# Experts with 96 rows: one strip of 64 array columns and one of 32 in place of three strips of 32

## The chip, the cores and the metric

The kernel runs on one core of a Trainium2 chip, with random inputs in float32. The metric is device time of one execution in microseconds (us), the median of several runs. TensorE (PE in the profile) is a 128x128 array; a matmul's stationary operand (loaded by LDWEIGHTS, PEld in the profile) may take all of its columns or a strip of them, and the strip is fixed by the PSUM partitions that the output goes to. In float32 each matmul of the program is two pairs of LDWEIGHTS and MATMUL in the trace, called passes here.

## The reference, cut to what matters

One decoder layer (projection, attention with forget gates, a chunked gating MLP, a merge, a mixture of experts, a gated per-layer embedding, a final norm) for 1024 prompt tokens and 64 sample tokens. The change lies in the mixture of experts:

```
# h: (1088, 1024); 32 experts in 4 groups; each token takes the best group and its best 2 of 8 experts
for each expert e, for its tokens x_e (counts differ by expert):
    y_e = (silu(x_e @ w_g[e]) * (x_e @ w_u[e])) @ w_d[e]   # 1024 -> 512 -> 1024
out[token] = sum of its two experts' rows, weighted
```

Each expert's weights are three matrices of 2 MB (w_g, w_u: 1024x512; w_d: 512x1024), so all 32 are 192 MB, read once.

## The kernel before, in words

The stages run one after the other: projection, attention, merge, routing, experts (`stage_moe`, from line 2213 on), a loop for rows that found no place (none of its matmuls is in this profile), and the final stage.

Routing ranks the experts by their number of rows. The 4 largest (`NSINGLE`) get a whole block of 128 rows. The next 12 (`NWIDE`) get 96 rows of a block each. The next six (`NSPLIT`) get 64 rows: 32 in each of two of those 12 blocks, in the strip that is left there (the lent strip). The last ten (`NHALF`) get half a block, 64 rows, two experts to a block. A block of 128 rows is a `Unit`: its list of strips (rank, first row, number of rows) covers the 128 rows. There are 21 units: 4 `single` (one strip of 128), 12 `wide` (96 rows of one expert and 32 of another) and 5 `halves` (two strips of 64).

For each unit, the block's rows are gathered, transposed on TensorE (line 2286) and kept as `XT`. The gate product, the up product (both through `product`, line 2292) and the two halves of the down product (line 2326) loop over the contraction in pieces of 128, called k-steps here (8, 8, and 2 times 4), and inside a k-step over the unit's strips:

```
for k in range(KD):
    for r, rows_ in strips(u):
        last = mm(out[rows_, :], XT[:, u % 2, k, rows_], c.ring_tile(LOAD[kind, r])[:, k, :],
                  start=(k == 0), stop=(k == KD - 1))
```

The stationary operand is the strip's rows of `XT` (128x32, 128x64 or 128x128), the moving one 128x512 of that strip's expert. So a strip of rows is a strip of array columns, and strips of one unit are different columns. A wide unit has four matmuls of 32 columns in each k-step; the first three have the same moving operand.

`ROUNDS` sets the order of the units: a single with a halves, then two wides, four times; then two rounds of two wides; then the last halves. In a round of units a and b TensorE's order is gate a, gate b, up a, up b, turn a (line 2312, transposes of the activation), transposes of the next round's rows, turn b, down a, down b. Weights come through a ring of 7 tiles of 2 MB; the SP queue issues a load (line 1837) when the last product that reads the tile's slot is done.

The code that the change touches:

Of the kernel before, what the change touches and what calls it, by code (L numbers as in the profile page):

```python
# [1765 lines left out]
STRIPE, HALF = P // 4, P // 2  # L1766
FIRST_SPLIT = NSINGLE + NWIDE
# [14 lines left out]
def wide(i, n):  # L1782

    r = NSINGLE + i + n * NSPLIT
    return Unit(r, [(r, STRIPE * q, STRIPE) for q in range(3)] + [(FIRST_SPLIT + i, 3 * STRIPE, STRIPE)])


def halves(i):
# [4 lines left out]
for _i in range(NSPLIT):  # L1793
    if _i < NSINGLE:
        ROUNDS.append([single(_i), halves(_i)])
    ROUNDS.append([wide(_i, 0), wide(_i, 1)])
# [1061 lines left out]
```

How the kernel before makes its waits and increments, by code:

```python
        @block.sync  # L213
# [2 lines left out]
                sp.dma_start(W[:, s], c.w_in[:, :, col:col + 512]).then_inc(c.w_in_sem[s], 16)  # L216
            for t in range(NP):
                sp.dma_start(X[:, t, :], c.x_prompt[t * P:(t + 1) * P, :]).then_inc(x_in[t], 16)
                if t == 1:
                    load_w(1, 2 * WA)
            sp.dma_start(X[0:NS, NP, :], c.x_sample).then_inc(x_in[NP], 16)
            load_w(0, 0)
            load_w(2, WA)
            load_w(3, OFF_U)
            sp.wait_ge(nb_done, H)
            for h in range(H):
                for b in range(DB):
                    sp.dma_start(c.sufd[h, b].rearrange("t (g k) -> g t k", k=32),
# [5 lines left out]
                sp.dma_start(c.g_ple[:], c.norm_ple_g).then_inc(c.consts_in, 16)  # L235
            sp.dma_start(c.w_route[:, :, 0:NG], c.w_router_group).then_inc(c.consts_in, 16)
            sp.dma_start(c.w_route[:, :, NG:], c.w_router_expert).then_inc(c.consts_in, 16)
            sp.dma_start(c.b_route[:, 0:NG], c.b_router_group).then_inc(c.consts_in, 16)
            sp.dma_start(c.b_route[:, NG:], c.b_router_expert).then_inc(c.consts_in, 16)
            sp.wait_ge(q_mm, NQ)
            sp.dma_start(W[:, 0], c.w_in[:, :, OFF_VB:OFF_VB + 512]).then_inc(c.w_vb_in, 16)
            for n, (out_p, out_s) in enumerate(((c.new_v_p, c.new_v_s), (c.new_k_p, c.new_k_s))):
# [5 lines left out]
        @block.gpsimd  # L248
# [25 lines left out]
            for t in range(NT):
                pool.wait_ge(ms_done, t + 1)
                g.tensor_tensor(c.stat[:, 2, t:t + 1], c.stat[:, 1, t:t + 1],
```

## Time and profile before

| | |
|---|---|
| median of 3 runs | 1864.62 us (1864.08 to 1866.16) |
| profiled execution, its time | 1865.02 us |
| profiled execution, its span | 1863.4 us |
| mean granted TensorE clock | 0.966 of full speed |
| PE busy | 1728.9 us, 93% of the span |
| expert stage | about 1193 to 1703 us of the span |

The span goes from the first to the last instruction of the program. Times inside the trace are counted from its start. The end of a matmul in the trace is modelled: a MATMUL of 512 columns is shown as 0.59 us long also where the next one on the same columns starts 0.43 us after it. So spacing is read from starts; the start of the last matmul in a merged row is the row's start plus its length less the length of one.

### The profile page before, as it was taken

The numbers are of one execution on the slowest core, as the hardware profiler recorded it, in microseconds if no ns is written. First come the engines' busy times: TensorE is split into PE (matmuls) and PEld (weight loads), VectorE is DVE, ScalarE is ACT, GpSimd is POOL, SyncE is SP. The second block draws the span as 40 slices with busy tenths as digits, with TensorE's granted clock in tenths as the row PEclk, the third lists the DMA queues.
The fourth block names the chain that finished last, engine by engine and source line by source line (L and its number), as shares of the span: only waits on it lengthen the run. The fifth ranks groups of instructions, "written<-read, shape, count | busy, mean of one in ns | idle before, by whom it ended". The sixth has DMA issues, their size and how long they took to land. (4 is left out here: it accounts for less than half of the span.)

```text
span 1863.4 us, 25932 instructions
## 1 busy us (share of the span) xinstructions
PE 1728.9 (93%) x10123; PEld 869.4 (47%) x10123; DVE 571.9 (31%) x1157; ACT 307.8 (17%) x567; POOL 194.3 (10%) x305
## 2 busy tenths in 40 slices
PE   7999999899999996998799997899998989994997
PEld 4564554556566663544455444433333333331443
DVE  4301104433334454565232226211111111101565
ACT  1000001222222222322110113200000000000122
POOL 2000004200000002333200000100000000001330
PEclk9999999999999998999999998899999999997999
DMA  8012110345344629999632144799999999998341
GB/s 287 5 13 93 49 51 1 107 150 172 119 170 159 229 94 316 351 377 353 239 146 79 65 167 158 282 415 427 427 426 428 426 427 425 428 427 331 113 150 65
DMA packets 132892, 426.11 MB, mean 229 GB/s; under 512 B 24137, under 2 KB 62602, under 8 KB 120482
## 3 DMA queue, kind: packets, MB, share of 16 engines
q1 hardware_dynamic: 97538, 326.94, 45.6%
q0 software_dynamic: 19344, 67.68, 9.9%
q10 hardware_dynamic: 15888, 29.83, 4.3%
q8 instruction: 81, 1.33, 0.3%
q14 instruction: 41, 0.34, 0.0%
HBM read 372.56 MB, written 51.84 MB: 228 GB/s over the span
## 5 line engine op out<-in xcount | busy, mean ns | idle before, releaser
L2292 PE MATMUL psum<-arena 128*32 128x512 f32 (+2 forms) x1984 | 304.1, 614 | 28.0 <-issue 25.1
L902 PE MATMUL psum<-arena 128*128 128x384 f32 (+1 forms) x768 | 253.9, 476 | 3.9 <-ACT arena L933 3.8
L2292 PEld LDWEIGHTS psum<-arena 128*32 128x32 f32 (+2 forms) x1984 | 103.0, 123 | 227.1 <-issue 226.4
L902 PEld LDWEIGHTS psum<-arena 128*128 128x128 f32 x768 | 139.8, 191 | 77.6 <-issue 6.1
L2326 PE MATMUL psum<-arena 128*32 128x512 f32 (+2 forms) x992 | 148.6, 594 | 1.0 <-DVE arena L2402 1.0
L2396 DVE TENSOR_TENSOR arena<-arena,psum 128x512 f32<-128x512 f32 x21 | 14.4, 688 | 410.5 <-PE psum L2292 410.5
L1692 PE MATMUL psum<-arena 128*128 128x512 f32 x256 | 114.7, 604 | 1.6 <-PEq L1513 1.6
L2654 PE MATMUL psum<-arena 128*128 128x512 f32 x256 | 114.0, 603 | 1.4 <-DVE arena L2680 1.4
L317 PE MATMUL psum<-arena 128*128 128x512 f32 x256 | 112.7, 597 | 0.0
L2326 PEld LDWEIGHTS psum<-arena 128*32 128x32 f32 (+2 forms) x992 | 46.9, 119 | 87.4 <-issue 86.1
L2370 ACT ACTIVATE arena<-psum 128x512 f32<-128x512 f32 x42 | 25.1, 597 | 319.5 <-PE psum L2326 319.5
L2654 PEld LDWEIGHTS psum<-arena 128*128 128x128 f32 x256 | 48.9, 194 | 60.4 <-issue 60.4
L1217 PE MATMUL psum<-arena 128*128 128x512 f32 x160 | 73.4, 601 | 2.6 <-DVE arena L1414 2.6
L1692 PEld LDWEIGHTS psum<-arena 128*128 128x128 f32 x256 | 48.2, 192 | 59.0 <-issue 59.0
L317 PEld LDWEIGHTS psum<-arena 128*128 128x128 f32 x256 | 48.4, 192 | 57.5 <-issue 57.5
L940 ACT ACTIVATE arena<-arena 128x128 f32<-128x128 f32 (+7 forms) x64 | 49.1, 768 | 143.8 <-DVE arena L1004 80.4
L1182 POOL DMA_DIRECT2D arena<-in_cache_v x112 | 60.3, 538 | 117.7 <-PE psum L1286 110.8
L1400 DVE STREAM_TRANSPOSE arena<-arena 128x2048 f32<-128x2048 f32 x27 | 61.8, 2299 | 19.5 <-DMA arena<-in_cache_k 19.5
L1892 POOL DMA_INDIRECT arena<-moe_in,arena x21 | 20.5, 975 | 445.4 <-PE psum L2286 399.9
L377 PE MATMUL psum<-arena 128*128 128x384 f32 (+1 forms) x192 | 58.7, 468 | 1.6 <-DVE arena L523 1.6
L342 PE MATMUL psum<-arena 128*128 128x384 f32 (+1 forms) x192 | 58.8, 469 | 0.0
L631 PE MATMUL psum<-arena 128*128 128x512 f32 x128 | 56.8, 598 | 1.7 <-PEq L212 0.9
(300 smaller groups left out, 1820.3 us busy)
## 6 DMA issues: line engine op xcount, KB each, us to landing
arena<-in_w_exp_gate SPq DMA_DIRECT2D x32, 2048.0 KB, 22.5
arena<-in_w_exp_up SPq DMA_DIRECT2D x32, 2048.0 KB, 23.2
arena<-in_w_exp_down SPq DMA_DIRECT2D x32, 2048.0 KB, 21.8
arena<-in_cache_v POOLq DMA_DIRECT2D x128, 256.0 KB, 9.2
arena<-in_cache_k SPq DMA_DIRECT2D x124, 256.0 KB, 8.3
arena<-in_w_in SPq DMA_DIRECT2D x24, 1024.0 KB, 6.1
moe_out<-arena POOLq DMA_DIRECT2D x5, 2560.0 KB, 11.6
moe_out<-arena ACTq DMA_DIRECT2D x21, 512.0 KB, 10.9
```

The source lines that it names most:

```text
L317: last = mm(c.bank[4 + r % 3][:, :], hidden_tile(HT, t)[:, k, :], W[:, n + 1, k, :], start=(k == 0), stop=(k == KD - 1))
L342: last = mm(c.bank[n % 4][:, 0:CUTS[sec + 1] - CUTS[sec]], W[:, 0, k, j * P:(j + 1) * P], HT[sec][:, k, :], start=(k == 0), stop=(k == KD ...
L377: last = mm(c.bank[4 + n % 3][:, 0:CUTS[sec + 1] - CUTS[sec]], W[:, 3, k, j * P:(j + 1) * P], HT[sec][:, k, :], start=(k == 0), stop=(k == ...
L631: last = mm(c.bank[t % 2][:, :], hidden_tile(HT, t)[:, k, :], W[:, 0, k, :], start=(k == 0), stop=(k == KD - 1))
L902: done = mm(c.bank[7][:, 0:b - a], WG[blk % 2][:, k, q * P:(q + 1) * P], HT[p // NCOL][:, k, :], start=(k == 0), stop=(k == KD - 1))
L1182: pool.dma_start(VC[:, ch, g, :], c.cache_v[bass.ds(numbers[ch][g] * P, P), :]).then_inc(v_in[ch], 16)
L1217: last = mm(c.bank[7][:, :], UP[col % 2][:, n, k, :], src[:, 4 * half:4 * half + 4, k, :], start=(k == 0), stop=(k == KF - 1))
L1400: v.transpose(keys, keys).then_inc(turned[b % 2], 1)
L1692: last = mm(c.bank[2 * (t % 2) + half][:, :], MT[:, k, t * P:(t + 1) * P], WO[:, k, half * 512:half * 512 + 512], start=(k == 0), stop=(k ...
L2292: last = mm(out[rows_, :], XT[:, u % 2, k, rows_], c.ring_tile(LOAD[kind, r])[:, k, :], start=(k == 0), stop=(k == KD - 1))
L2326: last = mm(y_ps[half][rows_, :], ACT_T[:, u % 2, k, rows_], c.ring_tile(LOAD["down", r])[:, k, cols], start=(k == 0), stop=(k == KF - 1))
L2654: last = mm(gate_ps[t % 2][:, half * 512:half * 512 + 512], XT[:, t % 2, k, :], c.wpg[half][:, k, :], start=(k == 0), stop=(k == KD - 1))
```

## The change

The strips of a wide unit are listed differently. The expert with 96 rows has one strip of rows 0 to 63 and one of rows 64 to 95; the lent strip, rows 96 to 127, stays. Nothing else differs: the same rows, blocks, weights, loads, order of units and semaphores.

```
--- before.py
+++ after.py
@@ -1782,7 +1782,7 @@
 def wide(i, n):
 
     r = NSINGLE + i + n * NSPLIT
-    return Unit(r, [(r, STRIPE * q, STRIPE) for q in range(3)] + [(FIRST_SPLIT + i, 3 * STRIPE, STRIPE)])
+    return Unit(r, [(r, 0, 2 * STRIPE), (r, 2 * STRIPE, STRIPE)] + [(FIRST_SPLIT + i, 3 * STRIPE, STRIPE)])
```

`STRIPE` is 32.

## Rows read from the trace of the kernel before

**Rows 1.** The page: the span, and TensorE's busy time, share and instructions.

```profile
span 1863.4 us, 25932 instructions
...
PE 1728.9 (93%) x10123; PEld 869.4 (47%) x10123; DVE 571.9 (31%) x1157; ACT 307.8 (17%) x567; POOL 194.3 (10%) x305
```

**Rows 2.** Windows by round: length, engines' busy us (instructions), TensorE clock, DMA share, GB/s.

```profile
1192.90:1240.30 47.40, 45.98 (x180) 19.77 (x184) 6.32 (x7) 4.08 (x6) 5.82 (x6) 1.00 0.83 324
1240.30:1285.00 44.70, 44.70 (x410) 15.02 (x408) 5.07 (x6) 3.58 (x6) 1.88 (x2) 1.00 1.01 427
1285.00:1330.00 45.00, 45.00 (x172) 18.25 (x168) 5.10 (x6) 3.58 (x6) 1.88 (x2) 1.00 1.01 426
...
1672.40:1702.50 30.10, 23.73 (x104) 8.99 (x100) 1.38 (x2) 1.79 (x3) 0.00 (x0) 0.94 1.02 416
sum 509.60, PE 481.28 PEld 179.25 DVE 52.26 ACT 38.13 POOL 19.91; mean PE 43.75 PEld 16.30 DVE 4.75 ACT 3.47 POOL 1.81
```

**Rows 3.** Chain that ended last, first wide round: start, us, what.

```profile
1240.32 27.60 PE psum L2292 x256
1267.92 0.68 PE psum L2312 x4
1268.60 0.89 PE psum L2286 x8
1269.49 0.48 PE psum L2312 x4
1269.97 3.57 PE psum L2326 x32
1273.54 1.09 PE psum L2286 x8
1274.63 10.44 PE psum L2326 x96
```

**Rows 4.** Waits of TensorE in the expert stage: us in total, times, longest.

```profile
PE psum L2292 <- issue: 25.1, 10, 4.6
```

**Rows 5.** Chain that ended last, last halves round.

```profile
1672.48 7.05 PE psum L2292 x32
1679.53 4.60 issue
1684.13 8.80 PE psum L2292 x32
```

**Rows 6.** Groups by line and form, TensorE, expert stage: busy us, mean ns, idle before.

```profile
L2292 PE MATMUL psum<-arena 128*32 128x512 f32 x1536 | 175.0, 616 | 17.8 <-issue 17.8
```

**Rows 7.** Timeline of TensorE, halves' down product to wide's gate: start, length, instructions.

```profile
1239.72 0.60 PE L2326 MATMUL psum<-arena 128*64 128x512 f32 x2
1240.25 0.64 PE L2292 MATMUL psum<-arena 128*32 128x512 f32 x4
...
1240.70 0.61 PE L2292 MATMUL psum<-arena 128*32 128x512 f32 x4
...
1241.13 0.61 PE L2292 MATMUL psum<-arena 128*32 128x512 f32 x4
```

**Rows 8.** Timeline of TensorE, wide's down product to halves' gate.

```profile
1671.87 0.61 PE L2326 MATMUL psum<-arena 128*32 128x512 f32 x4
1672.44 0.65 PE L2292 MATMUL psum<-arena 128*64 128x512 f32 x2
...
1672.89 0.63 PE L2292 MATMUL psum<-arena 128*64 128x512 f32 x2
```

**Rows 9.** Timeline of TensorE, attention of the samples: two changes of strip shape.

```profile
758.36 0.29 PE L1286 MATMUL psum<-arena 128*16 128x128 f32 x4
758.58 0.29 PE L1293 MATMUL psum<-arena 64*16 64x128 f32 x2
...
759.45 0.61 PE L1230 MATMUL psum<-arena 8*128 8x512 f32 x4
759.99 0.60 PE L1244 MATMUL psum<-arena 32*16 32x512 f32 x2
```

**Rows 10.** Timeline of TensorE, line 1286 with the steps ahead of its last one.

```profile
758.03 0.62 PE L1286 MATMUL psum<-arena 128*16 128x128 f32 x16
```

## The prediction

> **What bounds the kernel now.** I read the page first: TensorE is busy for 93% of the span [rows 1], so the question is what the change does to TensorE's time, in the one stage where it acts. The windows by round come next [rows 2]. The eleven rounds of experts take 509.6 us. In the rounds shown the DMA share is 1.01 or 1.02 at 416 to 427 GB/s from the second one on, and TensorE is busy for the whole of the first wide round (44.70 of 44.70 us). So two limits stand almost level here: the stream of weights and the matmuls. The waits show how level: TensorE sat idle for 25.1 us ahead of gate and up products, 10 times, with nothing behind it that the profile names [rows 4]; in a stage whose DMA is full I read this as weights that have not landed. A kernel that makes TensorE's work longer by x here therefore loses x less about 25 us, and one that makes it shorter gains next to nothing, because the weights still have to come.
>
> The first wide round of the chain of waits [rows 3] gives the parts: gate and up of both units 27.60 us, the down products 3.57 + 10.44 = 14.01 us, and transposes 0.68 + 0.89 + 0.48 + 1.09 = 3.14 us. The 256 matmul passes of gate and up are 4 products of 8 k-steps, each with 4 strips of 2 passes. So a k-step takes 27.60 / 32 = 0.86 us, two passes of 0.43 us: the four strips run beside each other, on disjoint columns, and each strip does its two passes one behind the other.
>
> **The change part by part.** It removes one matmul (two passes) in each k-step of the 12 wide units. A wide unit has 8 + 8 + 2 x 4 = 24 k-steps, so 288 k-steps in all (the 1536 passes of 32 columns at line 2292 are 12 x 16 x 8, which agrees [rows 6]), and 576 passes with their weight loads go, of 10123 [rows 1]. Their price now is nothing: they lie beside the other strips of the same k-step, whose two passes take 0.86 us anyway, and the strip of 64 needs two passes as well. DMAs, semaphores, gathers, evictions and the order of units stay; no wait is added and no queue is passed. So all depends on one thing: whether a strip of 64 columns and strips of 32 run beside each other as strips of one width do. No row of this kernel has two widths in one k-step, so I bound it from rows where one follows the other.
>
> The upper part of the bound is a change of width between products. When a wide unit's gate follows a halves' down product [rows 7], the last passes of 64 columns are two that start within 0.01 us (1239.72; the row is 0.60 long, one pass 0.59, so the later one starts at 1239.73), and the first of 32 starts at 1240.25: 0.52 us on, not 0.43. The next passes of 32 come 0.45 later (1240.70), and only then the pace is 0.43 (1241.13). In the other direction [rows 8] the last of 32 starts at 1671.87 + 0.61 - 0.59 = 1671.89, the first of 64 at 1672.44, 0.55 later, and the second at 1672.89, 0.45 later. So a change of width costs 0.09 to 0.12 us, and meanwhile nothing overlaps it.
>
> Does the change wait only for strips that share columns with the new one? In a mixed k-step none do, so this decides. Two places speak to it [rows 9]. At line 1286 four strips of 32 columns (16 used) with 128 rows run beside each other; line 1293 follows on the same four column strips, now with 64 rows. Its first matmul lies on columns 0 to 31, those of the strip that started first. It starts at 758.58. The four start between 758.36 and 758.36 + 0.29 - 0.27 = 758.38, so that is 0.20 after the last and 0.22 after the first. Passes of this form follow each other at (0.62 - 0.27) / 3 = 0.12 or a little less [rows 10], as 128 of 512 columns at the 0.43 pace would give 0.11; with the 0.09 of the change, 0.20. The same at line 1230, four strips of rows with 512 columns: the next shape, on the first strip of rows, starts at 759.99, 0.52 after the last (759.45 + 0.61 - 0.59 = 759.47) and 0.54 after the first. Both fit the constant counted from the last strip, though the new tile does not touch it. With rows of 0.01 us this is a hint and not a proof, but it says that a change of shape waits until the whole array has run empty.
>
> The Trainium skill, "TensorEngine Tiling (Array Packing)", section Tiling Modes, lists 128x64 and 128x32 as separate configurations and says that changing the mode, not just the tile, drains TensorE; by it every change of width in a k-step is such a drain, and the sum would be the one that follows. The 0.52 and 0.55 us of rows 7 and 8 bear it out for whole products; no run here shows it inside one.
>
> So I take: in each k-step the strip of 64 does its two passes alone, the array runs empty, the two strips of 32 do theirs together, and it runs empty again. A k-step is then 0.55 (change to 64) + 0.45 (second pass) + 0.52 (change to 32) + 0.45 (second pass) + 0.01 (stagger of the two strips) = 1.98 us in place of 0.86. A wide round has 48 k-steps: 95.0 us, and 3.14 of transposes, 98.2. Six of them: 589.1. The weights no longer hold anything up, since 9 loads of 2 MB at 427 GB/s take 44 us against 98 (estimate from rows 2): the idle time of rows 4 goes, and with it the slow clock behind it (8.80 us for a product that took 7.05 before the idle 4.60 [rows 5], in a round with a mean granted clock of 0.94 [rows 2]). Halves rounds then take what the undisturbed ones show: 47.40 for the first of the four with a single and 45.00 for each of the other three [rows 2], and 30.10 - 4.60 - 1.75 = 23.75 for the last round. The stage is 47.4 + 135.0 + 589.1 + 23.75 = 795.2 us against 509.6, 285.6 more. The span becomes 1863.4 + 285.6 = 2149.0. The profiled execution was 1865.02 long, 1.6 over its span and 0.4 over the median, so I forecast 2150 us. Its own range is 2130 to 2170: the two ends of the change's cost (0.52 for both, or 0.55 for both) move a k-step by 0.03 us, 9 us in all, and idle time of up to 10 us may stay in the halves rounds.
>
> **The rivals.**
>
> A. The widths overlap (not slower). Strips of a k-step lie on disjoint columns; if a pass is held only by passes on its own columns, the strip of 64 and the two of 32 each keep the 0.43 pace, the k-step stays at 0.86, and the time stays where it was: 1865 us, within 2 either way, because the weights pace the stage [rows 2, 4]. For it: each strip's chain of passes plainly runs on its own, since a strip's second pass comes only after the first passes of its neighbours although the code has it ahead of them. Against it: the starts of rows 9, counted from the last strip. It decides as soon as a change of width need not wait for disjoint columns. The Trainium skill, "TensorE: Matmul & The Clock Gate", Part 3, describes each 32x32 tile as able to hold other weights and work on another slice of the output, with tiles about 4 ns apart; by that the k-step would stay as it is. The page does not say this of tiles of two widths, and no run here shows it.
>
> B. The widths take turns, but rarely: TensorE already takes passes out of the code's order, and it may run many k-steps of the strip of 64 ahead before it turns to the strips of 32. Then a k-step costs its four passes one behind the other, 4 x 0.43 = 1.72, and few changes. A round is 82.6 + 3.1 = 85.7, the stage 47.4 + 135 + 514.2 + 23.75 = 720.4, 211 more: 2076 us. Against it: nothing shows how far ahead TensorE looks.
>
> C. The widths change at every pass (64, 32s, 64, 32s). A k-step is then 2 x 0.55 + 2 x 0.52 + 0.02 = 2.16, a round 106.8, the stage 847, 337 more: 2202 us. Against it: the second pass of the strip of 64 can start without a change when its first is through, 0.43 after it, before the array is empty.
>
> D. The widths overlap, but weights can't be loaded ahead, so each pass starts 0.52 after the one before. A k-step is 1.04, a round 53.1, the stage 524.6 without idle time: 1880 us.
>
> **How the numbers follow.** The forecast gets 0.60, B 0.10, C 0.08, A 0.14, D 0.04, anything worse or better 0.04. Faster or slower means by over 0.2%, 3.7 us, about what a measurement of this kernel can tell from no change. Slower holds the forecast, B, C, D and most of the rest: 0.86. A gives the 0.12 of no change and, as nothing is shortened that the weights don't pace, 0.02 of faster. The range goes from B to C with a little room, 2068 to 2206, and leaves out A, D and the rest.
>
> **What would show it.** In the timeline of a wide unit's gate, rows of 128*64 (one pass at a time) and 128*32 (two at a time) should alternate; the spacing from 64 to 32 should be 0.52 and from 32 to 64 up to 0.55, and a gate product should take about 15.9 us in place of 6.9. Passes of 32 columns at line 2292 should be 768, in place of 1536, and those of 64 should gain 384. The DMA share should fall well below 1 in wide rounds, and the idle time of rows 4 should nearly go. If passes of 64 and 32 start within 0.05 us of each other and the k-step is 0.86, the step "waits until the whole array has run empty" is wrong. If 64s come in long runs, B is right; if a 64 stands alone between two pairs of 32, C.

## The result, and the profile after

The changed kernel takes 2150.23 us (median of 4 runs, 2144.34 to 2152.55), the kernel before 1864.35 us in the same comparison. The ratio is 1.1526, with a 95% interval of 1.1506 to 1.1545. The forecast was 2150 us.

The page after, its span and TensorE's row: 576 passes fewer than in [rows 1], and 305 us more of busy time.

```profile
span 2142.7 us, 24780 instructions
...
PE 2034.1 (95%) x9547; PEld 883.6 (41%) x9547; DVE 571.7 (27%) x1157; ACT 307.6 (14%) x567; POOL 194.0 (9%) x305
```

The windows by round after, with the columns of [rows 2]. The first three rows are the same rounds as the first three there.

```profile
1186.98:1234.20 47.22, 45.81 (x176) 19.84 (x177) 6.32 (x7) 4.08 (x6) 5.81 (x6) 1.00 0.83 324
1234.20:1332.60 98.40, 98.40 (x315) 18.94 (x312) 5.09 (x6) 3.58 (x6) 1.87 (x2) 1.00 0.60 237
1332.60:1377.50 44.90, 44.90 (x171) 18.39 (x170) 5.10 (x6) 3.58 (x6) 1.87 (x2) 1.00 0.97 405
...
1958.20:1981.80 23.60, 21.78 (x102) 7.69 (x100) 1.38 (x2) 1.80 (x4) 0.00 (x0) 1.00 0.96 356
sum 794.82, PE 791.59 PEld 195.44 DVE 52.30 ACT 38.12 POOL 19.85; mean PE 71.96 PEld 17.77 DVE 4.75 ACT 3.47 POOL 1.80
```

A wide round went from 44.70 to 98.40 us, a round with a single and a halves stayed at 45 (44.90), and the DMA share of a wide round fell from 1.01 to 0.60: the weights have time to spare there. The granted clock is 1.00 (2.4 GHz) in every round.

The waits of TensorE in the stage after, in the columns of [rows 4]. The line of 25.1 us without a named releaser is gone, and these are all that is left.

```profile
PE psum L2292 <- DVE arena L2390: 2.8, 2, 1.4
PE psum L2326 <- DVE arena L2402: 1.0, 1, 1.0
PE psum L2312 <- DVE arena L2396: 0.8, 1, 0.8
```

Two k-steps of a wide unit's gate after, in the timeline of TensorE (start, length, instructions; the start is what counts). To be set beside the four strips at 0.43 in [rows 7].

```profile
1260.45 0.59 PE L2292 MATMUL psum<-arena 128*64 128x512 f32 x1
...
1260.97 0.62 PE L2292 MATMUL psum<-arena 128*32 128x512 f32 x2
...
1261.95 0.64 PE L2292 MATMUL psum<-arena 128*64 128x512 f32 x1
...
1262.43 0.59 PE L2292 MATMUL psum<-arena 128*64 128x512 f32 x1
```

The second pass of 64 columns starts at 1260.45. The two strips of 32 start together 0.52 later, do two passes, and the next pass of 64 starts at 1261.95, with its second at 1262.43. From second pass to second pass the k-step is 1.98 us, against 0.86. No pass of 64 lies beside one of 32, here or elsewhere in the stage: a pass of 32 follows one of 64 there 288 times and the reverse 285 times, and the start is never less than 0.52 us after the last one of the other width.

The weights of the new shape don't come early either. In the row of the weight loads (PEld) they start with its first pass, at 1261.95, 0.52 after the last pass of 32 (1261.43); without a change, in the kernel before, the loads for the passes at 1241.13 stand at 1240.70, beside the passes ahead.

```profile
1261.95 0.19 PEld L2292 LDWEIGHTS psum<-arena 128*64 128x64 f32 x2 [0.84 <-issue]
```

So these rows don't tell whether it is the pass or its weight load that waits.

### The profile page after: what moved, and what is told of

Read it like the earlier page. It is cut to its first block and busy times, and to the rows that moved or that the text cites. A ratio compares the mean times of both kernels' runs of the same rounds, so it can differ in the third digit from the quotient of the medians.

```text
span 2142.7 us, 24780 instructions
## 1 busy us (share of the span) xinstructions
PE 2034.1 (95%) x9547; PEld 883.6 (41%) x9547; DVE 571.7 (27%) x1157; ACT 307.6 (14%) x567; POOL 194.0 (9%) x305
## 5 line engine op out<-in xcount | busy, mean ns | idle before, releaser
L2292 PE MATMUL psum<-arena 128*32 128x512 f32 (+2 forms) x1600 | 508.3, 605 | 2.8 <-DVE arena L2390 2.8
L2292 PEld LDWEIGHTS psum<-arena 128*32 128x32 f32 (+2 forms) x1600 | 110.9, 126 | 397.7 <-issue 397.7
L2326 PE MATMUL psum<-arena 128*32 128x512 f32 (+2 forms) x800 | 255.3, 605 | 1.0 <-DVE arena L2402 1.0
L2326 PEld LDWEIGHTS psum<-arena 128*32 128x32 f32 (+2 forms) x800 | 55.2, 126 | 185.8 <-issue 184.4
L2370 ACT ACTIVATE arena<-psum 128x512 f32<-128x512 f32 x42 | 25.1, 597 | 514.0 <-PE psum L2326 514.0
L1400 DVE STREAM_TRANSPOSE arena<-arena 128x2048 f32<-128x2048 f32 x27 | 61.7, 2297 | 18.9 <-DMA arena<-in_cache_k 18.9
```

The costliest lines, as they stand in the source:

```text
L1400: v.transpose(keys, keys).then_inc(turned[b % 2], 1)
L2326: last = mm(y_ps[half][rows_, :], ACT_T[:, u % 2, k, rows_], c.ring_tile(LOAD["down", r])[:, k, cols], start=(k == 0), stop=(k == KF - 1))
```

## The experiments

Theory: a pass whose strip has another shape than those in flight waits until the whole array is empty, also when its columns are free; so strips of two widths never overlap, and each change costs on top. All runs are compared with the kernel before on the same chip.

**How the time follows the number of changes.** Two orders of the same matmuls, both in the changed kernel. The inner loops take their k-steps and strips from a list:

```
                ss = strips(u)                       # 64, 32, 32
                # e1_runs_of_64: 96 changes
                [(k, *ss[0]) for k in range(nk)] + [(k, *s) for k in range(nk) for s in ss[1:]]
                # e2_one_change_per_k: 288 changes
                [(k, *s) for k in range(nk) for s in (ss[1:] + ss[:1] if k % 2 else ss)]
```

> The changed kernel with another order inside a product: the strip of 64 does all its k-steps first, then the two strips of 32 do theirs together. Theory (a change of strip width waits until the whole array is empty, and widths never overlap): two changes per gate or up product and per half of down, 96 in all in place of 576. A change cost (1.985 - 4 x 0.4294) / 2 = 0.134 us in the changed kernel; 288 k-steps of 1.718 and 96 changes make 508 us, with 19 of transposes and 206 of the other rounds a stage of 732 against 797: 2088 us. Rival 1 (the price hangs on each pass of a unit with unequal strips, as its weights are not loaded ahead): the same number of passes, so 2150. Rival 2 (the widths could overlap if TensorE did not meet them so close in program order): not settled by this run.

> The changed kernel with the strip of 64 first in even k-steps and last in odd ones, so that one change of width falls to a k-step in place of two: 288 changes. Theory: 288 x 1.718 + 288 x 0.134 = 533 us, with 19 and 206 a stage of 758, 39 us less than with two changes: 2112 us, halfway between the changed kernel and the run with 96 changes within a few us. Rival 1 (price per pass): 2150.

Measured: 2085.84 us with 96 changes (ratio 1.1194, 1.1175 to 1.1213) and 2111.52 us with 288 (1.1343, 1.1317 to 1.1368), beside 2150.23 with 576. The stage, from its first gate pass to the end of its last down pass, took 732.1 and 758.2 us in the profiles (794.8 with 576). From 96 to 576 that is 62.7 / 480 = 0.131 us for a change; between 96 and 288 it is 0.136. Rival 1 falls: the passes are the same in number, and the time isn't. Carried back to no change at all (an estimate, no run has that) the stage is 732.1 - 96 x 0.131 = 719.5 us, still 210 over the 509.6 of [rows 2]: that is the overlap that the widths lose, 288 x 0.86 = 248 us, less what the weights give back.

**Is it the strip of 64, or the mixture?** The kernel before with wide units of two strips of 64, and with four strips of which two use half of their columns:

```
-    ... [(r, STRIPE * q, STRIPE) for q in range(3)] + [(FIRST_SPLIT + i, 3 * STRIPE, STRIPE)])
+    e3: [(r, 0, HALF), (FIRST_SPLIT + i, HALF, HALF)])
+    e4: [(r, 0, STRIPE), (r, STRIPE, STRIPE), (r, 2 * STRIPE, STRIPE // 2), (FIRST_SPLIT + i, 3 * STRIPE, STRIPE // 2)])
```

> The kernel before with wide units made of two strips of 64 (the 96-row expert's first 64 rows, and 64 columns of the lent expert); 32 rows of the wide expert are left out, and the lent expert's strip takes their place. The same weights are loaded. Theory: equal widths, so no change inside a product; k-step 0.86, 1864 us within 4. Rival (a strip of 64 beside a strip of another expert in a wide unit is what costs, whatever the width of the neighbour): over 2000.

> The kernel before with the third and the lent strip of each wide unit using 16 of their 32 columns; the other 16 rows of each are left out. Theory, if the shape that counts is the strip's place in steps of 32 columns and not the number of columns used: no change inside a product, k-step 0.86, 1864 us within 4. Rival (the number of columns of the loaded operand counts): two changes in each k-step, about 2150.

Measured: 1864.53 us (ratio 0.9996, 0.9982 to 1.001) and 1864.28 us (1.0001, 0.9991 to 1.001). So a strip of 64 beside another expert's strip costs nothing while that one is 64 too, and 16 used columns beside 32 are no change of shape: in the trace of e4 strips with 16 and with 32 columns start within 0.01 us of each other. Both rivals fall. e3 also removes half of a wide unit's matmuls. That its time stays the same doesn't show that they cost nothing, since the weights pace the stage; the gate and up products of its first wide round show it, with half of the passes in 27.47 us, where [rows 3] have 256 in 27.60:

```profile
1241.38 27.47 PE psum L2292 x128
```

**Rows count too, and disjoint columns don't help.** Four strips of 32 as before, the lent one over half of the contraction:

```
+            def contract(u, r):
+                return HALF if len(UNITS[u].strips) == 4 and FIRST_SPLIT <= r < FIRST_HALF else P
...
+                        p = slice(0, contract(u, r))
+                        last = mm(out[rows_, :], XT[p, u % 2, k, rows_], c.ring_tile(LOAD[kind, r])[p, k, :],
```

> The kernel before, four strips of 32 columns in a wide unit, but the lent strip contracts over 64 rows of the array in place of 128 (the other half of its contraction is left out). Theory in its wide form (any difference of a strip's shape, rows too, makes the array run empty; the line 1286 to 1293 rows are such a change): two changes in each k-step, three strips and then one, k-step 1.98, 2145 us within 15. Rival (only the number of columns counts): k-step 0.86, 1864 us.

Measured: 2143.53 us (1.1495, 1.1468 to 1.1522), a stage of 790.4 us. The timeline of TensorE in this run, one k-step and the start of the next; in a form like 64*32 the first number is the rows of the array, the second the columns:

```profile
1238.88 0.63 PE L2296 MATMUL psum<-arena 128*32 128x512 f32 x3
...
1239.34 0.61 PE L2296 MATMUL psum<-arena 128*32 128x512 f32 x3
...
1239.88 0.61 PE L2296 MATMUL psum<-arena 64*32 64x512 f32 x1
...
1240.33 0.59 PE L2296 MATMUL psum<-arena 64*32 64x512 f32 x1
...
1240.85 0.63 PE L2296 MATMUL psum<-arena 128*32 128x512 f32 x3
```

The lent strip sits on columns 96 to 127, which no other strip touches. The last of the other three starts at 1239.34 + 0.61 - 0.59 = 1239.36, and the lent strip's first pass waits until 1239.88, 0.52 on. Then the three wait for the lent one in turn, and from first passes to first passes the k-step is 1240.85 - 1238.88 = 1.97 us. That the array is empty at that moment is read from these starts, 0.52 after the last one whatever columns it is on; the trace only models where a matmul ends. This is what [rows 9] hinted at with differences of 0.02 us, now with a whole pass of 0.43 us at stake.

**How far TensorE looks ahead.** The kernel before with each strip's k-steps written one after the other, and the changed kernel without its strip of rows 64 to 95:

```
e6:  [(k, *s) for s in ss for k in range(nk)]          # four strips of 32
e9:  [(r, 0, 2 * STRIPE), (FIRST_SPLIT + i, 3 * STRIPE, STRIPE)]
```

> The kernel before, its four strips of 32 columns written one after the other: all k-steps of the first strip, then all of the second. It asks how far ahead TensorE looks for a pass on other columns, which decided between the forecast and the rival of rare turns. If it looks ahead over the 16 passes of a strip: k-step 0.86, 1864 us. If only over a pass or two, the strips of a product run one behind the other with a short overlap at each seam: 64 passes of 0.43 in place of 16 steps, 20.6 us more for each of 36 products, less some 35 of idle time and slow clock: about 2570 us. No theory of the shapes depends on it.

Measured: 2270.04 us (1.2174, 1.2146 to 1.2202), between the two. The windows of line 2297 (gate and up) in this run: length, busy (passes, those still running at the start included), clock, DMA share, GB/s.

```profile
1239.43:1244.60 5.17, 5.16 (x12) 1.00 0.99 414
1244.60:1246.32 1.72, 1.72 (x9) 1.00 1.02 431
1246.32:1249.78 3.46, 3.46 (x10) 1.00 1.03 438
```

The first strip does 12 of its 16 passes alone, one in 0.43 us. Then four steps hold two passes each (9, less the one still running): its passes 13 to 16 beside the next strip's first four. Then the second strip goes on alone for 8 (10 less two). So the next strip's first pass goes ahead when three earlier passes still wait, and not when four do. I had expected a pass or two at a seam; it is four of 16 in a gate or up product, and four of 8 in each half of down.

> The changed kernel without the strip of rows 64 to 95 (those rows are left out): a wide unit has the strip of 64 and the lent strip of 32. The run with the strips written one after the other showed a pass starting while three earlier ones of another strip still waited. In the changed kernel four passes of 32 stand between two k-steps' passes of 64; here only two, within that reach. Theory (a pass of another shape that waits for the empty array lets nothing pass it): two changes per k-step as before, 1.98 us, 2150 us within 8. Rival (TensorE lets the next k-step's passes of 64 go ahead of the waiting 32, so the widths take turns rarely): below 2130, down to 2085 as in the run with 96 changes.

Measured: 2148.87 us (1.1523, 1.1478 to 1.1568). Its timeline shows the changed kernel's alternation, although only two passes stand between two k-steps' passes of 64:

```profile
1240.99 0.64 PE L2292 MATMUL psum<-arena 128*64 128x512 f32 x1
...
1241.47 0.59 PE L2292 MATMUL psum<-arena 128*64 128x512 f32 x1
...
1242.00 0.62 PE L2292 MATMUL psum<-arena 128*32 128x512 f32 x1
...
1242.45 0.59 PE L2292 MATMUL psum<-arena 128*32 128x512 f32 x1
```

So nothing passed a pass that waited for the empty array; in these runs the look ahead works among strips of one shape only. The run also takes away one of two strips of 32 and saves nothing clear of its spread: the two ran side by side.

**What the weights give back.** The strip of 64 in the gate product alone, and in one of its k-steps alone:

```
-                    for r, rows_ in strips(u):
+                    for r, rows_ in (mixed(u) if kind == "gate" else strips(u)):               # e7
+                    for r, rows_ in (mixed(u) if kind == "gate" and k == 3 else strips(u)):    # e8
```

> The kernel before with the strip of 64 in the gate product alone: 96 mixed k-steps in place of 288. Theory with the credit of the weights (idle time and slow clock go once TensorE is the longer one): a wide round takes 44.5 + 16 x 1.123 = 62.5 us, the stage 206 + 375 = 581 against 510: 1936 us. Rival (no credit; the price adds to the time before): 96 x 1.123 = 108 more, 1972 us.

> The kernel before with the strip of 64 in a single k-step of the gate product of each wide unit: 12 mixed k-steps, 13.5 us of TensorE's time. Theory (the weights pace the stage, TensorE has some 25 to 35 us to spare there): hidden, 1864 to 1868 us. Rival (TensorE sets the time in the wide rounds as they are): 1878 us.

Measured: 1936.27 us (1.0381, 1.0362 to 1.04) and 1864.82 us (1.0000, 0.999 to 1.0009). With 96 mixed k-steps, 36 of 108 us are given back, and the waits without a named releaser are gone in its profile. With 12, all 13.5 are. The waits of TensorE in the run with 12, where [rows 4] have 25.1 us:

```profile
PE psum L2298 <- issue: 16.2, 8, 4.6
```

## Why the prediction was right

- "The strips removed cost nothing now." Right: e3 leaves out half of the passes of a wide unit, and its gate and up products take 27.47 us in place of 27.60.
- "A change of shape waits until the whole array has run empty." Right, and the step on which all hung. Before, it rested on 0.02 us in two places; e5 shows it on columns that nobody else uses, e1 and e2 show that the time follows the number of changes. Whether the pass or its weight load does the waiting stays open.
- The k-step of 1.98 us: right, the timeline has 1.98. Its parts were cut differently. The change to 64 took 0.52 and not 0.55, and the second pass of 64 came 0.48 after the first and not 0.45; the sum of the two was 1.00 in both. The 0.55 of [rows 8] was misread as the price of a change: there the weight load of the new width starts at 1672.41, 0.52 after the last pass of 32, its first pass 0.03 after that, and the second pass 0.48 after the load. So both directions cost 0.52, and the 0.12 was no upper end.
- The wide round: 98.2 forecast, 98.40 measured; the stage 795.2 against 794.8; the last round 23.75 against 23.60.
- The credit of some 36 us for idle time and slow clock (288 x (1.98 - 27.60 / 32) = 322 us of longer k-steps, of which the sum keeps 285.6): right, the stage grew by 794.8 - 509.6 = 285.2. The waits are gone, the clock is 1.00 in every round, and e7 and e8 meet the same credit at two smaller doses.
- Rival A (overlap) falls with the timeline and e5. B (rare turns) falls with the timeline; e9 says why, a pass that waits for the empty array is not passed. C (a change at every pass) and D (overlap without early loads) fall with the same rows: the passes come in pairs of a width, and none lies beside another width.

The agreement of the median to 0.2 us is partly luck. The profiled execution took 2144.34 us, six below the median, and its expert stage began at 1187.0 of the span where that of the kernel before began at 1192.9: 5.9 us come from the stages ahead, which the change doesn't touch. The run at the median left no trace, so that its stage took 794.8 us too is not shown.

No version here beats the kernel before. With equal shapes the stage is paced by its weights: e3 and e4 take the same time, and the other order of equal strips (e6) costs time.

## What to carry to other kernels

In every pair tried here (64 columns and 32, 128 rows and 64, in float32) strips ran beside each other only when they had one shape, in columns and in rows, so give them one; the strips of 32 that look redundant (three with the same moving operand) are what keeps a unit of 96 + 32 rows at the price of one strip. Where widths must be mixed, gather the passes of one width into runs: here a change costs 0.13 us, and the lost overlap 0.86 us for each k-step, which no order tried here brought back. Not tried: to mirror the strips of one of a round's two units, and interleave the two, so that passes of 64 of both could lie beside each other. And before counting removed instructions as a gain, see in the timeline whether they ever stood in line or only beside others.

## What the runs showed of the hardware that was not expected

- Passes do not start in program order: one on other columns goes ahead of up to three that wait (e6). That fits [rows 7], where the first passes of all four strips start before any second one. At a change of shape this ends (e9).
- The shape that counts is the size of the strip's place in the array, not the columns in use: 16 used of a strip of 32 cost nothing (e4), 64 rows in place of 128 cost about as much as another width (2143.53 against 2150.23 us).
- After a change the first pass of a strip of 64 columns is followed by its second after 0.48 us, one of 32 after 0.45, and then at 0.43; so of the 0.13 us that a change costs, 0.09 lie in the wait for the empty array and 0.02 to 0.05 in the pass after it. The wider strip pays more, which fits its longer weight load (135 ns against 108 on average after the change) that starts only with the pass; no run takes the two apart.
